# Weighting and adding the two chosen expert rows of each token by TensorE products with diagonals

## The reference, cut to what matters

```python
    tw = jax.nn.softmax(tv, axis=-1) * gw
    eid = gi[..., None] * EXPERTS_PER_GROUP + ti
    dense_w = jnp.sum(jax.nn.one_hot(eid, N_EXPERTS, dtype=jnp.float32) * tw[..., None], axis=-2)
    ...
    return jnp.einsum('bsef,efd->bsd', act, lp['moe_w2'])
...
    x = x + gate2 * hier_moe(h2, lp)
```

## Time and profile before

| | |
|---|---|
| median of 3 runs | 1787.7 us (1785.29 to 1788.49) |
| the profiled execution, its own time | 1786.96 us |
| its span in the trace | 1785.1 us |
| mean granted TensorE clock | 0.975 of full speed |
| tail of layer 0 in the span | about 891 to 922 us |
| tail of layer 1 in the span | about 1754 us to the end |

### The profile page before, as it was taken

The page is one execution under the profiler, slowest core; times in us unless marked ns, Lnnn a source line. Parts: engine busy times, 40 slices in busy tenths (PEclk is TensorE's granted clock), DMA queues, the critical chain, the costliest instruction groups (busy, mean ns, idle before and its releaser), DMA issues.

```text
span 1785.1 us, 33890 instructions
## 1 busy us (share of the span) xinstructions
PE 1632.4 (91%) x13289; PEld 1103.4 (62%) x13289; DVE 1172.5 (66%) x1877; ACT 891.5 (50%) x1477; POOL 475.7 (27%) x434
## 2 busy tenths in 40 slices
PE   5899989999999996999889999899999899879995
PEld 3478766777765565544466886677776655645444
DVE  4495354777734847988566916477774385589974
ACT  4322555666642122878543236366665411358874
POOL 0223243112232212223143315321122411222213
PEclk8899999999999998999989999999999999999998
DMA  9565435532235554999945542232223275389975
GB/s 328 184 213 180 156 133 198 192 122 78 65 119 203 186 204 173 383 404 407 333 164 168 189 167 94 77 105 78 75 78 105 100 266 219 118 302 404 405 307 195
DMA packets 191627, 351.49 MB, mean 197 GB/s; under 512 B 15795, under 2 KB 99314, under 8 KB 191218
## 3 DMA queue, kind: packets, MB, share of 16 engines
q1 hardware_dynamic: 182005, 320.17, 50.6%
q0 software_dynamic: 7776, 28.32, 4.3%
q10 hardware_dynamic: 1693, 0.89, 0.2%
HBM read 288.32 MB, written 61.01 MB: 196 GB/s over the span
## 4 chain that ended last, share of the span: by engine, by line
PE 66%; DVE 11%; DMA 8%; ACT 6%; issue 5%; DVEq 2%; SPq 1%; ACTq 1%; POOL 1%; POOLq 0%
PE PS L445 39%; PE PS L452 12%; PE PS L1193 3%; PE PS L1177 3%; DMA arena<-in_moe_w 3%; DMA y_rows<-scratch 3%; PE PS L963 2%; DVE arena L2591 2%; PE PS L928 1%; PE PS L945 1%; DMA arena<-in_c_wukv 1%; SPq L783 1%; ACT arena L1617 1%; PE PS L995 1%; DMA hpart<-h_rows,wulo 1%
## 5 line engine op out<-in xcount | busy, mean ns | idle before, releaser
L1909 POOL TENSOR_TENSOR wlo<-wf,whi 128x256 f16<-128x256 f32 (+1 forms) x276 | 294.1, 1099 | 850.5 <-ACT whi L1533 800.0
L445 PE MATMUL PS<-hpart,whi 128*128 128x320 f16 x2048 | 423.7, 300 | 19.0 <-ACT arena L1617 17.8
L445 PE MATMUL PS<-hpart,wlo 128*128 128x320 f16 x1024 | 306.7, 299 | 0.0
L445 PE MATMUL PS<-whi,hpart 128*128 128x256 f16 (+2 forms) x1536 | 285.0, 286 | 11.2 <-DVE hpart L2790 7.3
L445 PEld LDWEIGHTS PS<-hpart,whi 128*128 128x128 f16 x2048 | 190.2, 98 | 108.8 <-issue 39.8
L445 PE MATMUL PS<-wlo,hpart 128*128 128x256 f16 (+2 forms) x768 | 217.8, 286 | 0.0
L445 PEld LDWEIGHTS PS<-whi,hpart 128*128 128x128 f16 x1536 | 148.0, 98 | 65.8 <-issue 26.9
L2397 DVE TENSOR_REDUCE stat<-PS 128x1 f32<-128x640 f32 (+1 forms) x160 | 110.6, 712 | 80.2 <-PE PS L1177 77.6
L1617 ACT ACTIVATE arena<-PS,pcol 128x320 f32<-128x320 f32 x128 | 67.5, 527 | 167.9 <-PE PS L445 162.8
L452 PE MATMUL PS<-hpart,whi 128*128 128x128 f16 (+1 forms) x768 | 139.5, 305 | 12.4 <-DVE hpart L2072 10.8
L2225 DVE SCALAR_TENSOR_TENSOR scratch<-scratch,cw 128x655 f32<-128x655 f32 x120 | 138.8, 1198 | 4.8 <-issue 0.4
(11 more groups left out here) (368 smaller groups left out, 2851.5 us busy)
## 6 DMA issues: line engine op xcount, KB each, us to landing
arena<-in_moe_w SPq DMA_DIRECT2D x68, 1024.0 KB, 13.7
arena<-in_w_ada SPq DMA_DIRECT2D x48, 1024.0 KB, 7.9
wf<-in_w_gate SPq DMA_DIRECT2D x32, 1024.0 KB, 6.0
wf<-in_moe_w SPq DMA_DIRECT2D x28, 1024.0 KB, 13.2
g_rows<-arena SPq DMA_DIRECT2D x128, 160.0 KB, 1.8
wf<-in_w_in SPq DMA_DIRECT2D x18, 1024.0 KB, 9.5
y_rows<-scratch SPq DMA_DIRECT2D x34, 512.0 KB, 12.1
arena<-g_rows SPq DMA_DIRECT2D x24, 640.0 KB, 5.0
```

Of the source, the lines that this page charges most:

```text
L445: ins = pe.matmul(out, st, mv, start=first and n == 0, stop=last and n == 2)
L1909: ins = pool.tensor_tensor(lo[:, a:b], wf[j][:, a:b], hi[:, a:b], ALU.subtract)
```

## The change

ACT no longer scales whole rows and nobody adds. Instead ACT builds, once per layer, ten diagonal matrices of 128x128: the identity times the weight column of a tile and a choice (`wdiag`). PE multiplies a 128x128 piece of the gathered rows, as the stationary operand, by the diagonal, as the moving one. That turns the piece and weights it in one step; the product of the second choice is accumulated on that of the first in PSUM. Eight transposes a tile become sixteen float32 products. The three idle products after each of tiles 1 to 4 go; the six after tile 0 stay. ACT's muls of the rows, DVE's `combined` and POOL's adds go, with `ybuf` in this part. PE now waits for the gathers itself, and once for the diagonals. DVE's loop is one step shorter; `modulation` keeps its place between `added(3)` and `added(4)`.

```diff
+        wdiag = [arena[:, o:o + 640].rearrange("p (t n) -> p t n", t=TILES) for o in (11264, 15360)]
...
-                    pe.wait_ge(*(comb_ready(l, tile + 1) if tile < 2 else comb_pool(l, tile - 1)))
+                    pe.wait_ge(*cg_in[tile](l, 32))
                     if tile >= 2:
                         pe.wait_ge(*x2_ready(l, tile - 1))
                     elif ahead:
                         pe.wait_ge(*bias_ready(l + 1, 8))
+                    if tile == 0:
+                        pe.wait_ge(*wd_ready(l, 1))
                     for k in range(KC):
-                        ins = pe.transpose(PS[:, tile % 2, k * P:(k + 1) * P], ybuf[tile % 2][:, k * P:(k + 1) * P],
-                                           ident[:, :])
+                        for ch, rows in enumerate((cga, cgb)):
+                            ins = pe.matmul(PS[:, tile % 2, k * P:(k + 1) * P], rows[:, tile, k * P:(k + 1) * P],
+                                            wdiag[ch][:, tile, :], start=ch == 0, stop=ch == 1)
                     ins.then_inc(yt_done.sem, 1)
...
-                    if step < TILES:
-                        if step:
-                            idle(3, 2 * ((step - 1) % 2))
-                        else:
-                            idle(6)
+                    if step == 0:
+                        idle(6)
...
                 rows_back(p * 2 + 4, 0, p + 2)
+                for tile in range(TILES):
+                    for ch in range(2):
+                        ins = act.mul(wdiag[ch][:, tile, :], ident[:, :], rcol[:, 5 + ch, tile:tile + 1])
+                ins.then_inc(wd_ready.sem, 1)
                 act.activation(stat[:, 2, 15:16], epsc[:, :], ACT.Sqrt)
...
                 for step in range(TILES + 4):
-                    if step < TILES:
-                        act.wait_ge(*cg_in[step](l, 32))
-                        if step >= 2:
-                            act.mul(cgb[:, step, :], cgb[:, step, :], rcol[:, 6, step:step + 1])
-                        act.mul(cga[:, step, :], cga[:, step, :], rcol[:, 5, step:step + 1]).then_inc(ca_ready.sem, 1)
...
-                for tile in range(2, TILES):
-                    pool.wait_ge(*ca_ready(l, tile + 1))
-                    pool.wait_ge(*yt_done(l, tile - 1))
-                    pool.tensor_tensor(ybuf[tile % 2], cgb[:, tile, :], cga[:, tile, :], ALU.add).then_inc(comb_pool.sem, 1)
...
-                def combined(tile):
-
-                    dve.wait_ge(*ca_ready(l, tile + 1))
-                    dve.scalar_tensor_tensor(out=ybuf[tile % 2], in0=cgb[:, tile, :], scalar=rcol[:, 6, tile:tile + 1],
-                                             in1=cga[:, tile, :], op0=ALU.mult, op1=ALU.add).then_inc(comb_ready.sem, 1)
-
...
-                for step in range(TILES + 2):
-                    if step < 2:
-                        combined(step)
-                    if 0 <= step - 1 < TILES:
-                        added(step - 1)
-                    if l + 1 < LAYERS and step == 4:
+                for step in range(TILES + 1):
+                    if step < TILES:
+                        added(step)
+                    if l + 1 < LAYERS and step == 3:
                         modulation(l + 1, 0)
-                    if l + 1 == LAYERS and 0 <= step - 2 < TILES:
-                        final_rows(step - 2)
+                    if l + 1 == LAYERS and step:
+                        final_rows(step - 1)
```

More of the change, by code:

```diff
@@ L432, in build @@
         first_in = Signal(cg_in[0].sem, 48)
-        ca_ready = sig("ca_ready", TILES)
-        comb_ready = sig("comb_ready", 2)
-        comb_pool = sig("comb_pool", TILES - 2)
+        wd_ready = sig("wd_ready", 1)
         yt_done = sig("yt_done", TILES)
```

## The result

| | before | the change |
|---|---|---|
| median, us | 1788.1 (1785.29 to 1789.91, 4 runs) | 1799.15 (1797.92 to 1801.62, 4 runs) |
| profiled execution, own time / span | 1786.96 / 1785.1 | 1798.56 / 1796.7 |
| mean granted clock | 0.975 | 0.977 |

The ratio to before is 1.0065, with a 95% interval of 1.0048 to 1.0082: slower by 11.6 us, and the two profiled executions are 11.6 apart as well (the medians 11.05). The forecast was 1800.0, within 1794 to 1806.

The account below looks back on a forecast made before the run. PE, busy 91% of the span, was taken to set the pace in layer 0's tail, ACT and POOL in most of layer 1's. Tails of +8.0 and +4.5 us make +12.5 on 1786.96, 1799.5; given as 1800.0, range 1794 to 1806.

Parts of the forecast that it names:

- The price of a product: On PE: two passes of 0.113 us each, so a tile takes 3.6 us in place of 0.87, 2.7 more.
- Tail of layer 0: First tail, from the diagonals through the five tiles to the last sum: +8.0 us in all.
- The diagonals: Layer 0: ten ACT instructions ahead of `ada_copy` take 2.4 us; with the clock, tile 0 starts +2.0 us later.
- Five tiles and three groups of idle products: Layer 0 on PE: five tiles of +2.7 us each, +13.5; three idle groups of 1.4 go, -4.1.
- Behind tile 4: Layer 0, between tile 4 and the last sum: 3.5 us in place of 5.5, with `modulation` run earlier; -2.0.
- The last sum: End of layer 0's tail: at full clock after a shorter wait, 1.8 us in place of 3.2; -1.4.
- Tail of layer 1: Second tail, from PE's earlier start through the tiles to the end: +4.5 us in all.
- tile 0 with six idle products: Layer 1: 8.7 us in place of 6.0, the clock rising 5.1 us after PE's start; +2.7.
- tiles 1 to 4: Layer 1: PE sets the pace, 17.0 us in place of 12.2; +4.8.
- One pass: Rival, both tails: a product costs one pass of 0.109, a tile 1.75 us; about 1784 in all; chance 0.04.
- four passes: Rival, both tails: 64 instructions and 7.2 us a tile; about 1836 in all; chance 0.02.
- The falling clock: Rival, layer 0: without idle products the lower clock comes from tile 1 on; about 1819 in all; chance 0.04.

Follow-up runs that it names:

- diag_late: The change with the ten diagonals made after the two casts and `ada_copy` instead of ahead of them; 1.0041 of the kernel before, 4.3 us less than the change.
- before_mod_first: The kernel before with `modulation` of layer 0's tail moved ahead of the first `combined`; 1.0002 of the kernel before.
- diag_late_no_idle6: `diag_late` without the six idle products behind tile 0, so none stand between tiles; 1.0027 of the kernel before, 2.5 us less than `diag_late`.
- new_one_choice: The change with the first choice's products alone, the second choice's rows left out; 0.9988 of the kernel before, 13.8 us less than the change.
- transposes_only: The change with eight transposes of the first choice's rows replacing the sixteen products, no weights or second choice; 0.9973 of the kernel before.
- new_layer0: The kernel before with the change in layer 0's tail alone, the old tail in layer 1; 1.0039 of the kernel before, 7.0 us more.

## Why the prediction was right, point by point

**The price of a product** was right and carries the result: two passes, 32 a tile, 3.57 us (3.68 where tile and sum follow each other) for a forecast 3.6, from rows of three other kinds of product. Spacing is 0.112, at the lower bound. By the rule of the Trainium skill (FP8 and Floating Point Precision, Matmul Precision), four passes to a true float32 product, a tile would have shown 64 records; it shows 32, and the measurement decides.

**Tail of layer 0**, forecast +8.0, measured +8.7:
- *The diagonals*, forecast +2.0 for the start of tile 0, measured +0.9 (19.2 against 18.4 after the copy). ACT took more than thought, 2.93 for ten in place of 2.4; the nearest row had 0.32 us, an `ACTIVATE` with a per-partition scale takes 0.39. PE's idle products began 3.5 later. But the clock rose at 891.69, not at 894.93 or later, and gave most of it back. `diag_late` shows what the place costs when the clock doesn't help, 2.5.
- *Five tiles and three groups of idle products*, +13.5 and -4.1: tile 4 starts 41.39 after the copy, before 33.85, 7.5 more; less the 0.9 at the start that is 6.7, exactly four tiles of 2.7 less 4.1.
- *Behind tile 4*, forecast 3.5: from the end of the products (923.5) to the last sum (926.97) 3.5. `modulation` ran while PE was at tile 4 and POOL had finished, as short as in `before_mod_first`:

```profile
896.75 8.39 POOL L1907 TENSOR_TENSOR wlo<-wf,whi 128x1024 f16<-128x1024 f32 x4
...
920.39 0.17 DVE L2127 TENSOR_TENSOR ada<-adan,pcol 128x16 f32<-128x16 f32 x1
```

  This 2.0 comes from POOL's adds being gone, so the prediction's sentence that they are worth nothing in layer 0 contradicts its own term. `before_mod_first` gets the same 2.0 without any of the change.
- *The last sum*, forecast 1.8 at the higher clock: this step failed in the profiled execution. It took 3.6, the clock fell 1.2 us before it:

```profile
891.69:925.82 34.13, 32.97 (x264) 32.06 (x264) 11.13 (x43) 4.81 (x5) 12.22 (x9) 1.00 0.29 110
925.82:942.89 17.07, 11.09 (x40) 6.99 (x41) 9.69 (x27) 5.79 (x12) 0.00 (x0) 0.50 0.43 154
```

  I had reasoned from the length of PE's wait alone. Of the six experiments with products in layer 0, five had it at 1.96 to 1.98, and `diag_late_no_idle6` again at 3.6. `spread` stayed at 2.5 in all.

The two clock terms missed by -1.1 and +1.8 and nearly cancelled; the sum was right partly by that.

**Tail of layer 1**, forecast +4.5, measured +3.5: start 2.5 earlier, as forecast; tile 0 with six idle products 7.7 for 8.7, since the clock rose 3.0 us after PE's start, not 5.1 (2.1 us sooner, where the prediction named 1.7 as the bound, which no row had given); tiles 1 to 4 16.9 for 17.0; the end 0.4 shorter for 0.5.

**The rivals.** One pass and four passes fell with the count of records. The falling clock did not come between the products: 1.00 from 891.69 to 925.82. But the lower clock is real with transposes. In the two kernels without the three idle products it came at 902.56 and 912.06 and stayed beyond the end of the tail, at least 25.8 and 19.3 us of it; in the two with them in which it fell early it stayed 6.8 and 3.4 us, and in the kernel before it didn't fall between the tiles at all. So the idle products seem to bring the clock back; that they keep it from falling isn't shown. The Trainium skill's remark (TensorE: Matmul & The Clock Gate, Part 4) that transposes do not count as PE being busy in the same way agrees with these runs: eight transposes and a sum a tile lost the clock, sixteen products and a sum kept it, and so did eight (`new_one_choice`). They don't separate it from the mere amount of work, 0.9 us a tile against 3.6 and 1.8, nor from PE's waits for ACT, of 0.6 to 2.15 us, which ended 0.6 to 2.9 us before each of the four early falls.

That the muls and DVE's adds were worth nothing in layer 0 stays argued from the chain: `transposes_only` has none of them and a first tail no shorter than before, but it started tile 0 2.9 us later and lost the clock as well. In layer 1 they were worth 3.6 us (34.4 against 38.1), and the products took 7.1 for them (41.6).

## What to carry to other kernels

Work moved onto the engine that already sets the pace costs its full price, whatever it frees elsewhere; a float32 product costs two passes where a transpose costs one, and two products a piece make that four. Price it from any row of the same kind in the trace, with the count of records as well as their length. Where idle products stand between short work on PE, measure what the clock does without them before they are counted as free time, and do not count on a clock level in the last microseconds before a change of pace.

## What the runs showed of the hardware that was not expected

- A pass of a float32 product takes the same 0.112 us with 128 moving columns as with one; only at 148 it is 0.125.
- `modulation` of 128x16 on DVE took 1.86 us beside POOL's casts, and 0.22 and 0.17 away from them (`before_mod_first`, the change).
- Two kernels with the same instructions in the first tail, the change and `new_layer0`, lost the clock 47.4 and 50.3 us after ACT's copy (925.82 - 878.43, 926.74 - 876.40), and their tails are 59.5 and 57.7. That is as much as some of the edits here were worth. With one trace of each, it isn't shown whether the kernel or the single execution decides it. A gain of 3.3 us behind tile 4 was lost almost whole ahead of it in `before_mod_first`, where PE waited and the clock fell in between.
